# Forty-eight 128x128 transposes on TensorE rewritten as products with the identity matrix

## The reference

```python
mod = (c @ w_ada + b_ada)               # adaLN rows: shift, scale and gate of each block
h = rmsnorm(x) * (1 + sc1) + sh1
proj = h @ w_in                         # q, k, v, z, b, a, latents, branch gates
y_a = gdn_branch(...)                   # delta rule: chunked for the prompt, recurrent for samples
y_b = mla_branch(...)                   # latent attention over the prompt, over paged caches for samples
x = x + g1 * ((sigmoid(ga) * y_a + sigmoid(gb) * y_b) @ w_out)
x = x + g2 * moe_ffn(rmsnorm(x) * (1 + sc2) + sh2)      # top 4 of 32 experts
y = rmsnorm(x) * (1 + mod_f[1]) + mod_f[0]
```

## Time and profile before

| | us |
|---|---|
| median of 3 runs | 1583.73 |
| lowest, highest of the 3 | 1583.39, 1586.76 |
| the profiled execution, its own time | 1582.66 |
| span of its trace | 1580.8 |
| TensorE busy | 1505.3 (95%) |
| VectorE busy | 486.1 (31%) |
| ScalarE busy | 332.7 (21%) |
| HBM traffic over the span | 342 GB/s |

### The profile page before, as it was taken

The page is one execution under the profiler, slowest core; times in us unless marked ns, Lnnn a source line. Parts: engine busy times, 40 slices in busy tenths (PEclk is TensorE's granted clock), DMA queues, the critical chain, the costliest instruction groups (busy, mean ns, idle before and its releaser), DMA issues.

```text
span 1580.8 us, 24567 instructions
## 1 busy us (share of the span) xinstructions
PE 1505.3 (95%) x9785; PEld 786.8 (50%) x9785; DVE 486.1 (31%) x1130; ACT 332.7 (21%) x792; POOL 6.8 (0%) x13
## 2 busy tenths in 40 slices
PE   5999899999999999999999999999999999999996
PEld 4888885776577686433333333333333333333332
DVE  2655566322301024322221222222212212222224
ACT  2333452222311102111111111111111111111113
POOL 0000000000000000000000000000000000000000
PEclk9998999999999999999999999999999999999999
DMA  9848442635399975699999999999999999999994
GB/s 396 335 160 336 210 163 90 227 134 166 128 327 361 342 307 196 258 385 427 428 429 429 428 428 428 429 429 428 428 428 429 429 428 428 429 428 429 428 428 181
DMA packets 60162, 541.31 MB, mean 342 GB/s; under 512 B 7202, under 2 KB 11810, under 8 KB 29250
## 3 DMA queue, kind: packets, MB, share of 16 engines
q1 hardware_dynamic: 59378, 534.65, 82.0%
q0 software_dynamic: 720, 5.76, 0.9%
HBM read 533.54 MB, written 6.84 MB: 342 GB/s over the span
## 4 chain that ended last, share of the span: by engine, by line
PE 60%; DMA 32%; DVE 5%; issue 2%; ACT 1%; SPq 0%; ACTq 0%; DVEq 0%
DMA ring<-w_gu 31%; PE banks L567 16%; PE banks L1338 9%; PE banks L613 6%; PE banks L881 5%; PE banks L1163 2%; PE banks L541 2%; PE banks L1095 2%; DMA ring<-wpre 1%; PE banks L979 1%; PE banks L814 1%; PE banks L1188 1%; PE banks L1365 1%; PE banks L1223 1%; PE banks L1383 1%
## 5 line engine op out<-in xcount | busy, mean ns | idle before, releaser
L567 PE MATMUL banks<-ring,regA 128*64 128x512 f32 x2024 | 451.1, 595 | 16.4 <-DMA ring<-w_gu 16.4
L567 PEld LDWEIGHTS banks<-ring,regA 128*64 128x64 f32 x2024 | 140.8, 137 | 303.0 <-issue 264.1
L613 PE MATMUL banks<-ring,regC 128*64 128x512 f32 x1024 | 226.8, 595 | 1.4
L675 DVE TENSOR_TENSOR regB<-regB,banks 128x528 f32<-128x528 f32 x128 | 81.5, 698 | 327.6 <-PE banks L541 327.6
L613 PEld LDWEIGHTS banks<-ring,regC 128*64 128x64 f32 x1024 | 71.6, 137 | 136.0 <-issue 127.8
L641 ACT ACTIVATE regA<-regA 128x512 f32<-128x512 f32 x32 | 20.2, 630 | 532.2 <-DVE regA L697 532.2
L697 DVE TENSOR_SCALAR regA<-banks 128x512 f32<-128x512 f32 x32 | 22.1, 691 | 350.9 <-PE banks L584 350.9
L516 PE MATMUL banks<-regC,regA 128*64 128x512 f32 (+1 forms) x396 | 99.7, 622 | 1.0 <-DVE regA L667 1.0
L881 PE MATMUL banks<-hT,ring 128*128 128x264 f32 x384 | 86.5, 387 | 0.0
L881 PEld LDWEIGHTS banks<-hT,ring 128*128 128x128 f32 x384 | 72.6, 190 | 12.8 <-issue 0.4
L541 PE MATMUL banks<-regA,regC 64*128 64x264 f32 x512 | 71.6, 409 | 0.0
(11 more groups left out here) (514 smaller groups left out, 1534.5 us busy)
## 6 DMA issues: line engine op xcount, KB each, us to landing
ring<-w_gu SPq DMA_DIRECT2D x126, 2048.0 KB, 23.7
ring<-w_dn SPq DMA_DIRECT2D x64, 2048.0 KB, 21.6
ring<-wpre SPq DMA_DIRECT2D x41, 2048.0 KB, 13.3
ring<-kvT SPq DMA_DIRECT2D x64, 256.0 KB, 4.6
ring<-kv SPq DMA_DIRECT2D x64, 256.0 KB, 6.3
ring<-ssm SPq DMA_DIRECT2D x2, 2048.0 KB, 11.7
o_ssms<-ring POOLq DMA_DIRECT2D x2, 2048.0 KB, 7.8
regC<-w_gu SPq DMA_DIRECT2D x1, 2048.0 KB, 12.0
```

Source lines behind the costliest of these rows:

```text
L567: mm = pe_mm(bank[x // 2][SLOT * (x % 2):SLOT * (x % 2 + 1), :], lhsT=hg[:, k % 4, SLOT * (k // 4):SLOT * (k // 4 + 1)], rhs=weights_k[:, ...
L613: mm = pe_mm(bank[5][SLOT * y:SLOT * (y + 1), :], lhsT=actT[:, m % 4, SLOT * (m // 4):SLOT * (m // 4 + 1)], rhs=ring[c][:, D * (m % 4) + H ...
L675: V.tensor_tensor(pair, pair, banks[:, b:b + 2, 0:T], ALU.add).then_inc(acc_added, 1)
```

## The change

Both helpers that turn a block now call the ordinary product instead of the transpose: the block is the stationary operand, the identity matrix the moving one, and each product starts and stops its own accumulation. Places, order, banks, semaphores and all other turns of the kernel (among them those of the expert loop) stay as they are.

```diff
             def turn_mod(i, b, at=0):
                 pe.wait_ge(mod_row, i + 1)
-                pe.transpose(bank[b][:, at:at + P], mrow[:, i % 2, :], ident).then_inc(mod_turned, 1)
+                pe_mm(bank[b][:, at:at + P], lhsT=mrow[:, i % 2, :], rhs=ident, start=True, stop=True).then_inc(mod_turned, 1)
...
                     for i in range(4):
-                        mm = pe.transpose(bank[2 + g][:, i * P:(i + 1) * P], qkvT[:, H * (1 + w) + 4 * g + i, tok], ident)
+                        mm = pe_mm(bank[2 + g][:, i * P:(i + 1) * P], lhsT=qkvT[:, H * (1 + w) + 4 * g + i, tok], rhs=ident, start=True, stop=True)
                     mm.then_inc(tr_ready, 1)
```

## The result

The changed kernel takes 1591.48 us (median of nine executions, 1587.76 to 1595.35) against 1582.97 us for the kernel before (nine executions, 1579.73 to 1586.76): a ratio of 1.0050, with an interval of 1.0037 to 1.0062, or 8.5 us slower. The forecast was 1584.4 us, between 1582.3 and 1587.3, and no change that can be told. It missed the size by more than a factor of ten.

What follows compares the result with a forecast made beforehand. The prediction took TensorE's order to bound the run up to the experts, then the weight transfers, which start when TensorE arrives. L971's 0.40 and L820's 0.30 us on the median 1583.73 gave 1584.4 us, range 1582.3 to 1587.3.

Steps and rivals of the forecast that it cites:

- the price of a product: In a stream of 128x128 products, a product replacing a turn was to cost 2 to 3 ns more per instruction.
- The first of the prediction's own signs of being wrong: In the changed kernel's trace, a burst longer than 0.9 us would mean more passes and a wrong prediction.
- the sum: Added cost on TensorE's path: 0.40 us for eight L971 bursts, 0.30 for L820 turns, together +0.70 us.
- A product pays four passes: Rival: 40 turns on the path each cost 0.33 us more, 13 us in all, 1597 us; chance 0.03.
- The start of a burst: Bursts of L971 and L820 behind smaller pieces of the array each grow by 0.05 us, elsewhere by nothing worth counting.
- That what is lost ahead of the experts reaches the end: Expert weight transfers start once TensorE reaches the experts, so gains or losses at 150 to 225 us shift the end equally.
- The cover of the other eight turns: Eight of L820's sixteen turns lie under other waits and cost nothing; uncovered, 0.05 us each, 0.40 in all.
- The waits called issue: Rival: the 1.64 us delta-rule wait at 175.84 vanishes or doubles, giving 1582.8 to 1586.1 us; chance 0.13.
- The bound that I gave for their lower end: If delta-rule waits at 175.84 and 216.82 ignore TensorE's progress, they swallow work ahead; two bursts remain, 0.10 us.
- the first rival: The clock falls in the delta rule for one more stretch, 3.4 us more, 1587.8 us; chance 0.09.

Runs made afterwards that it cites:

- L820 alone: The kernel before with only the 16 turns of L820 as products, L971 left as transposes: 1585.11 us against 1584.02, ratio 1.0015.
- the doubled products: The changed kernel with each product of L971 issued twice: 1593.00 us against 1584.02 for the kernel before, ratio 1.0047.
- L971 alone: The kernel before with only the 32 turns of L971 as products, L820 left as transposes: 1585.60 us against 1584.02, ratio 1.0015.

## Why the prediction was wrong

**The step that failed is the price of a product, in the second paragraph of the part on costs.** It read the eight L947 pieces of 0.89 us as eight products and set 0.111 us against the turn's 0.11. They are four products. `products` calls L947 for four heads in each of two groups and two halves, 16 times, and the earlier trace rows give it 32 records, while L971 is called 32 times and has 32. The count was in the rows, and dividing records by calls would have shown it: an fp32 product is two passes of 0.111 us, a transpose one of 0.109. The exchange in a stream costs 0.11 us a turn, not 2 to 3 ns. The first of the prediction's own signs of being wrong, a burst longer than 0.9 us, is what the trace shows: 1.16.

The same slip runs through the burst: four L1035 records of 0.71 us are two products. Four products take 0.71 + 4 x 0.112 = 1.16 us, which is what the changed kernel shows. Set against the turns' 0.66 that is +0.50 a burst and +4.0 us for eight, where the sum had +0.40. For L820, the chain's pieces of the eight turns on the path grow by about 1.0 us together (0.26 to 0.42 at 149.86 and its successor at 150.43, 0.37 to 0.64 for each pair, 0.11 to 0.22 in the stream), where the sum had 0.30. The direct cost is about 5 us instead of 0.70, by the trace; the runs do not show that all of it reaches the end.

**The rival had it.** "A product pays four passes" was named, with 0.19 us a step as the point from which it decides; the step is 0.22. It is two passes, not four, so its price of 13 us was too high, and its chance, 0.03, came from the same misread 0.89 us. The Trainium skill, "Perfetto Trace Analysis", section Transposes, which asks for transposes, was right for this kernel: the form with two passes is 0.5% slower. A pass of either form takes about 0.11 us, so what shows here is the number of passes and not arithmetic that is skipped. The Trainium skill, "TensorE: Matmul & The Clock Gate", section Terms, has transpose mode 4x faster for fp32; here it is 2x, 0.109 us against 0.223, and the measurement decides.

**The start of a burst** was right as a mechanism: the first pass of a product behind smaller pieces takes 377 ns against 329, and the burst grows by 0.05 us for it.

**That what is lost ahead of the experts reaches the end** was right: 944.04 and 944.05 us from the first expert product to the end, with the transfers as they were.

**The cover of the other eight turns** did not hold in full: the changed kernel's chain has three more of them, a second one near 32 us and those at 138.52 and 144.01. What they cost is not shown; L820 alone costs 1 to 2 us in all.

**The waits called issue** were seen, given 0.13, and dismissed as no change that a measurement can tell. That was the second error. The direct 5 us leave some 3.5 of the 8.5. 32 instructions without work, ahead of the delta rule, take 3.7 us off, and behind it nothing, so a part of the loss seems to hang on where the code lies and not on what it computes. The bound that I gave for their lower end, that such a wait swallows work ahead of it, is in part what the doubled products showed: 7.1 us of passes more, 3.7 more in the corrected figure, and 0.4 us of issue waits left.

**The clock** did what the first rival said, in part. The wait grew from 1.64 to 2.31 us, and the clock stood at 0.57 from 181 to 185 us behind it. In five of the sixteen traces such a fall stands behind an issue wait of 2.25 to 2.78 us in the delta rule. But falls stand there behind waits of 0.9 to 1.7 us too, among them in the run with 32 instructions ahead, and none behind waits of 1.88 and 2.23 us, so a longer wait does not by itself bring one. One stretch withheld about 1.7 us and not 3.4, since it was half as long as the one of the earlier trace rows, and over all executions the clock withheld 1.3 to 2.2 us more than before, which at 0.70 is 0.9 to 1.5 us.

Put together: 5.0 us of passes, 0.9 to 1.5 of clock, and 0.2 to 2.8 us of longer issue waits (6.0 and 3.4 us in the changed kernel's two traces, 3.2 in before's): 6.1 to 9.3 around the measured 8.5. The means over all executions agree: the changed kernel's 15 lie 7.9 us above before, 1.1 of it with the clock and 6.7 without; the eight with 32 instructions ahead lie 4.5 above, -0.3 with the clock and 4.8 without, about the passes alone. So of what those instructions took off some 1.4 us is clock and some 1.9 is not, the latter about twice its standard error. The sum is an account and not a proof: with L971 alone only 2.6 of the 4.0 us of passes came through. What stays open is what exactly ends an issue wait, and why the single pieces differ between two executions of the same kernel; that they are waits for instructions is argued from the transfer ahead of them and from the runs that move the code, not shown by a record of the wait itself. Nor is it shown how much of the clock's share follows from the waits.

## What to carry to other kernels

Before a row prices an operation, divide its records by the calls in the code: an operation that the program expands shows as a harmless duration with a doubled count. An fp32 turn in TensorE should stay a transpose; as a product with the identity it takes two passes instead of one, and the second can cost wherever TensorE's order is the path. In this kernel 32 instructions without work, ahead of a stretch of many small matmuls, went with 3.7 us less, so a difference of a few us in such a stretch needs a control with the code shifted, and the time that the clock withheld beside it, before it is put down to the change.

## What the runs showed of the hardware that was not expected

An fp32 product of 128x128 stands in the trace as two weight loads of 192 ns and two passes of 275 ns, 0.112 us from start to start at full clock; a transpose is one load of 140 ns and one pass of 272 ns. The Trainium skill, "FP8 and Floating Point Precision", section Matmul Precision, has four passes for true fp32; the records here show two. In which of the page's modes these products run, no run shows.

32 instructions that do nothing went with 3.7 us less out of 1590 when they stood ahead of the delta rule, and with nothing less when they stood behind it (+8.5, +5.7, +4.8 us for 0, 16 and 32 ahead; +9.2 for 32 behind); in the kernel before they changed nothing that can be told. The Trainium skill, "Advanced Engine Details and Errata", section "Sequencer and Instruction Queues", under ISA Cache, gives the instruction cache a line of 16 KB, which it puts at 256 instructions. The trace agrees with the 16 KB (queue q8 of the kernel before moves 0.75 MB in 46 instruction transfers); how many instructions that is, and whether places in such blocks are what the shift changes, no run here shows.

The granted clock accounts for most of the scatter of this kernel: 0.70 us of span for each us withheld (a correlation of 0.90), over 90 executions of the kernel before, whose spans go from 1576.7 to 1587.2 us with granted clocks from 0.995 down to 0.986.
